# Six tiles of the last projection as three Strassen pairs, between the steps of the sample attention

## The reference, cut to what matters

```
u = rmsnorm(x, norm_w) @ w_in
cq = rmsnorm(u[..., :Q_LORA_RANK], q_norm_w)
gate = u[..., Q_LORA_RANK:]
...
o_lat = mla_attend(q_lat, q_pe, q_pos, c_kv, k_pe, k_pos)
o = jnp.einsum('bthr,rhv->bthv', o_lat, kv_w_uv).reshape(B, T, MLA_GATE_WIDTH)
return x + (o * jax.nn.silu(gate)) @ w_out
```

## Time and profile before

| | |
|---|---|
| median of 3 runs | 1011.04 us (1010.95 to 1015.64) |
| profiled execution, first to last instruction | 1015.5 us |
| TensorE busy | 989.5 us, 97% of the span, 4180 matmul records |
| VectorE, ScalarE, GpSimd busy | 54%, 40%, 43% |
| mean granted TensorE clock | 0.992 |

### The profile page before, as it was taken

How to read it: one execution, slowest core, us unless ns; L and a number is a source line. 1 busy time by engine, 2 the same in 40 slices (tenths; PEclk the granted TensorE clock), 3 DMA queues, 4 the chain that set the end, 5 groups by cost and what they waited for, 6 DMA issues and landing times.

```text
span 1015.5 us, 11585 instructions
## 1 busy us (share of the span) xinstructions
PE 989.5 (97%) x4180; PEld 620.6 (61%) x4180; DVE 548.5 (54%) x1087; ACT 411.2 (40%) x803; POOL 437.0 (43%) x404
## 2 busy tenths in 40 slices
PE   7999999999979999999999999999999999999998
PEld 4666776767645453634546777777666666656655
DVE  5974573755667686877756333253244535443225
ACT  3476877765774635536221000011222423243221
POOL 1576785976524858677321263111530302100110
PEclk9999999999998999999999999999999999999999
DMA  7215234334285999999898122212211111303202
GB/s 274 76 68 182 85 109 158 109 129 140 86 322 218 371 411 369 395 357 380 338 349 306 61 83 83 83 42 107 80 59 35 51 42 45 120 7 127 81 27 103
DMA packets 45576, 164.22 MB, mean 162 GB/s; under 512 B 4996, under 2 KB 8200, under 8 KB 36560
## 3 DMA queue, kind: packets, MB, share of 16 engines
q1 hardware_dynamic: 45520, 163.49, 43.5%
HBM read 106.25 MB, written 57.23 MB: 161 GB/s over the span
## 4 chain that ended last, share of the span: by engine, by line
PE 66%; DVE 2%; POOL 1%; ACT 1%; issue 1%; DMA 0%; SPq 0%; ACTq 0%; POOLq 0%; DVEq 0%
PE work_a L764 6%; PE work_a L1118 6%; PE work_b L1327 5%; PE work_b L764 5%; PE bank L1202 5%; PE work_b L1411 5%; PE work_a L1094 4%; PE bank L1085 3%; PE work_b L1070 3%; PE work_a L1011 3%; PE work_b L1202 3%; PE bank L1372 2%; PE work_a L1397 2%; PE work_a L1357 1%; PE bank L1524 1%; PE work_a L1202 1%
## 5 line engine op out<-in xcount | busy, mean ns | idle before, releaser
L2704 POOL TENSOR_TENSOR arena<-arena 128x640 f32<-128x640 f32 x96 | 138.8, 1463 | 38.6 <-ACT arena L1563 36.1
L2314 DVE SCALAR_TENSOR_TENSOR arena<-arena,bank 128x512 f32<-128x512 f32 x128 | 87.1, 742 | 38.2 <-PE bank L1085 38.2
L2878 POOL COPY arena<-arena 32x640 f32<-32x640 f32 x20 | 16.9, 846 | 123.1 <-ACT arena L1867 116.8
L886 PE MATMUL work_a<-arena 128*128 128x320 f32 x224 | 66.5, 441 | 2.0 <-DVE arena L2079 2.0
L886 PE MATMUL work_a<-arena,ring 128*128 128x320 f32 x224 | 64.9, 432 | 0.0
L1118 PE MATMUL work_a<-arena 128*128 128x512 f32 x128 | 64.1, 613 | 0.0
L886 PE MATMUL work_b<-arena 128*128 128x320 f32 x224 | 62.9, 433 | 0.0
L764 PE MATMUL work_a<-arena,ring 128*128 128x320 f32 x192 | 55.8, 451 | 7.2 <-DMA ring<-in_stream 7.2
L886 PEld LDWEIGHTS work_a<-arena 128*128 128x128 f32 x224 | 43.2, 193 | 20.6 <-issue 3.3
L886 PEld LDWEIGHTS work_b<-arena 128*128 128x128 f32 x224 | 42.9, 191 | 18.0 <-issue 0.4
L886 PEld LDWEIGHTS work_a<-arena,ring 128*128 128x128 f32 x224 | 42.3, 190 | 17.3
(11 more groups left out here) (359 smaller groups left out, 2047.6 us busy)
## 6 DMA issues: line engine op xcount, KB each, us to landing
ring<-in_stream SPq DMA_DIRECT2D x66, 512.0 KB, 3.6
arena<-in_c SPq DMA_DIRECT2D x32, 1024.0 KB, 8.8
out_s_c<-arena SPq DMA_DIRECT2D x32, 1024.0 KB, 7.0
arena<-in_keys SPq DMA_DIRECT2D x8, 664.0 KB, 4.0
z_scratch<-arena SPq DMA_DIRECT2D x16, 320.0 KB, 2.9
v_scratch<-arena SPq DMA_DIRECT2D x20, 256.0 KB, 2.3
k_scratch<-arena SPq DMA_DIRECT2D x4, 1280.0 KB, 5.4
arena<-k_scratch SPq DMA_DIRECT2D x4, 1280.0 KB, 9.1
```

Of the source, the lines that this page charges most:

```text
L886: last = mm(quarter[q], weights[:, k, :], tokens_of[:, k, :], start=fresh and k == 0, stop=k == KH - 1, skip_group_check=True)
L2314: op = v.scalar_tensor_tensor(ct[s % CS][:, g, :], ct[s % CS][:, g, :], decb[:, h, b:b + 1], bank[g][:, :], ALU.mult, ALU.add)
L2704: op = g.tensor_tensor(dst, dst, parts[(adds[0] - adds[1]) % len(parts)], ALU.add)
```

## The change

Tiles 0 and 1 stay as they are (16 k-steps). Tiles 2 to 7 become three pairs m = 1, 2, 3. In a pair the two weight tiles (w0, w1), each split into upper and lower four k-tiles, and the tokens, split at frame 256, form 2 x 2 blocks. Seven products of 4 k-steps at 256 columns take the place of 2 x 8 k-steps at 512 columns. Their names in the order of issue: FIRST, SECOND, OTHER, THIRD, FOURTH, FIFTH, SEVENTH. FIRST and OTHER add up in one half of `work[1]`; otherwise the products take turns between the two halves, so that a product waits until DVE has read the one two before it.

- TensorE: `last_products` is a generator, `fill(n)` takes n k-steps from it. The iterations b = 1 to 6 hand out 5 + 5 k-steps where they handed out 3 + 3; b = 0 hands out 3 + 1 of tiles 0 and 1 and 2 of pair 1; then 8 and 14.
- POOL: `mix_last_weights(m)` makes four sums of weights (128 x 512 each) for a pair: for pair 1 before `keep_own(0)`, for pairs 2 and 3 in the iterations b = 3 and b = 5, behind `keep_own(b + 3)`. `mix_last_tokens` makes four differences of tokens (128 x 1024 each) once: the first needs the upper four tiles of `og`, the others wait until DVE has written all of `og` (`E.free[0]` at 24). It stands between `keep_own(0)` and `keep_own(1)`.
- DVE: `took_last` takes the six results of a pair from PSUM and adds them to `x1` at two or more places; ten instructions for a pair where there were two. ACT: `keep_first(m)` copies FIRST to SBUF before OTHER is added to it. Squares wait for a new signal of a finished tile.

The core of the diff (`last_part`, semaphore sums and buffer places left out):

```diff
-        out_after = {0: (0, 1), 1: (2,), 3: (3,), 4: (4,), 5: (5,)}
+        squares_after = {0: (0, 1), 2: (2,), 3: (3,), 5: (4,), 6: (5,)}
+        took_after = {1: ((1, L_SECOND), (1, L_OTHER)), 2: ((1, L_THIRD), (1, L_FOURTH)), 3: ((1, L_FIFTH), (1, L_SEVENTH)),
+                      4: ((2, L_SECOND), (2, L_OTHER)), 5: ((2, L_THIRD), (2, L_FOURTH), (2, L_FIFTH)), 6: ((2, L_SEVENTH),)}
+        mixed_after = {3: 2, 5: 3}
...
+                for m in range(1, N_STRASSEN + 1):
...
+                    yield from product(m, L_FIRST, w0[:, upper], og[:, upper, left])
+                    if m == 1:
+                        pe.wait_ge(O.free[1], c.all(O.free[1]))
+                        pe.wait_ge(last_mixed, LAST_MIXED + TOKENS_MIXED + 4)
+                    else:
+                        took(m - 1, L_SEVENTH)
+                    pe.wait_ge(last_mixed, LAST_MIXED + W_MIXED[m - 1] + 2)
+                    yield from product(m, L_SECOND, last_w_mix[1], last_x_mix[1])
+                    pe.wait_ge(last_kept, LAST_KEPT + m)
+                    yield from product(m, L_OTHER, w0[:, lower], og[:, lower, left], False)
+                    took(m, L_SECOND)
+                    yield from product(m, L_THIRD, last_w_mix[0], last_x_mix[0])
+                    pe.wait_ge(last_mixed, LAST_MIXED + W_MIXED[m - 1] + 4)
+                    took(m, L_OTHER)
+                    yield from product(m, L_FOURTH, last_w_mix[3], og[:, lower, right])
+                    took(m, L_THIRD)
+                    yield from product(m, L_FIFTH, last_w_mix[2], last_x_mix[2])
+                    took(m, L_FOURTH)
+                    yield from product(m, L_SEVENTH, w1[:, lower], last_x_mix[3])
...
             for b in range(STREAMS - 1):
                 sample_scores(b + 1)
-                out_calls(3)
+                if b:
+                    fill(5)
+                else:
+                    out_calls(3)
                 sample_turn(b)
-                out_calls(3)
+                if b:
+                    fill(5)
+                else:
+                    out_calls(1)
+                    fill(2)
                 sample_outputs(b)
             sample_turn(STREAMS - 1)
-            out_calls(4)
+            fill(8)
             sample_outputs(STREAMS - 1)
-            out_calls(6)
+            fill(14)
...
+            def mix_last_tokens():
...
+                g.tensor_tensor(last_x_mix[0], top_y[:, :, right], top_y[:, :, left], ALU.subtract).then_inc(last_mixed, 1)
+                pool.wait_ge(E.free[0], 6 * PAIRS)
+                pool.wait_ge(last_mixed, LAST_MIXED + TOKENS_MIXED + 1)
+                g.tensor_tensor(last_x_mix[1], low_y[:, :, right], last_x_mix[0], ALU.subtract).then_inc(last_mixed, 1)
+                g.tensor_tensor(last_x_mix[2], low_y[:, :, right], top_y[:, :, right], ALU.subtract).then_inc(last_mixed, 1)
+                pool.wait_ge(last_mixed, LAST_MIXED + TOKENS_MIXED + 2)
+                g.tensor_tensor(last_x_mix[3], low_y[:, :, left], last_x_mix[1], ALU.subtract).then_inc(last_mixed, 1)
...
+                    pool.wait_ge(out_w_in, 16 * (KD - SLOTS))
+                    pool.wait_ge(last_mm, last_done(m - 1, L_FIFTH))
...
-            for b in range(3):
-                keep_own(b)
+            pool.wait_ge(gate_mm, GATE_MM * (PAIRS - 1))
+            pool.wait_ge(rotated, c.all(rotated) + PAIRS)
+            pool.wait_ge(E.free[0], 6 * (PAIRS - 1) + 2)
+            mix_last_weights(1)
+            keep_own(0)
+            mix_last_tokens()
+            keep_own(1)
+            keep_own(2)
             for b in range(STREAMS):
-                for t in out_after.get(b, ()):
+                for t in squares_after.get(b, ()):
                     add_out_square(t)
                 if b + 3 < STREAMS:
                     keep_own(b + 3)
+                if b in mixed_after:
+                    mix_last_weights(mixed_after[b])
```

More of the change, by code:

```diff
@@ L382, in program @@
         uv = take(RT, AH * P)
+        pe_at = top[0]
         pe_raw = take(T)
@@ L1305, in _ @@
             out_order = iter([(t, k) for t in range(2) for k in range(KD - 2)]
[L1306 to L1307 removed]
+                             + [(t, k) for t in range(2) for k in (KD - 2, KD - 1)])
             def out_calls(n):
@@ L1314, in out_calls @@
                     if k == 0:
[L1315 to L1324, removed]
+                        slot = 2 + t
+                        pe.wait_ge(w_in[slot], c.next(w_in[slot], step=16))
+                        pe.wait_ge(E.free[1], c.all(E.free[1]))
+                        pe.wait_ge(gate_out, GATE_OUT * (PAIRS - 1))
                     if t == 0 and k >= KD - 2:
@@ L1331, in out_calls, with last_products, product, took @@
                         c.skip(O.free[w])
+            def last_products():
+                upper, lower, left, right = slice(0, KH), slice(KH, KD), slice(0, QUARTER), slice(QUARTER, SEQ)
+                def product(m, which, weights, tokens_of, fresh=True):
+                    for k in range(KH):
+                        last = mm(last_part(m, which), weights[:, k, :], tokens_of[:, k, :], start=fresh and k == 0,
+                                  stop=k == KH - 1, skip_group_check=True)
+                        if k == KH - 1:
+                            last.then_inc(last_mm, 1)
+                        yield
+                def took(m, which):
+                    pe.wait_ge(last_took, last_read(m, which))
+                for m in range(1, N_STRASSEN + 1):
+                    if m == 1:
+                        w0, w1 = ring[:, 0], ring[:, 1]
+                        for slot in range(2):
+                            pe.wait_ge(w_in[slot], c.next(w_in[slot], step=16))
+                        pe.wait_ge(O.free[0], c.all(O.free[0]))
+                    else:
+                        w0, w1 = out_w[:, 2 * m - 4], out_w[:, 2 * m - 3]
+                        pe.wait_ge(out_w_in, 16 * (KD - SLOTS))
+                        took(m - 1, L_FIFTH)
+                    yield from product(m, L_FIRST, w0[:, upper], og[:, upper, left])
+                    if m == 1:
+                        pe.wait_ge(O.free[1], c.all(O.free[1]))
[15 more added lines that the diff above has]
+                    yield from product(m, L_SEVENTH, w1[:, lower], last_x_mix[3])
@@ L1333, in stage_e, with fill @@
+            last_calls = last_products()
+            def fill(n):
+                for _ in range(n):
+                    next(last_calls)
             def stage_e(p):
@@ L1526, in _ @@
                         pe.wait_ge(out_summed, c.all(out_summed, ahead=KD - 1))
-                        pe.wait_ge(O.free[0], c.all(O.free[0]))
+                        pe.wait_ge(last_took, last_read(N_STRASSEN, L_SEVENTH))
                         op = mm(work[1][:, 0:SEQ], ones_f[:], out_sum, start=True, stop=True)
@@ L2594, in _ @@
                 own_probabilities((b + 1) % 2)
-                for t in out_after.get(b, ()):
-                    add_out(t)
+                if b == 0:
+                    add_out(0)
+                    add_out(1)
+                for m, which in took_after.get(b, ()):
+                    took_last(m, which)
                 keep_sample(b)
-            add_out(KD - 2)
+            for m, which in last_took_early:
+                took_last(m, which)
             keep_sample(STREAMS - 1)
-            add_out(KD - 1)
+            for m, which in last_took_late:
+                took_last(m, which)
             for g in range(2):
@@ L2928, in _, with mix_last_weights @@
                     mix_gate_weights(p)
+            def mix_last_tokens():
+                left, right = slice(0, QUARTER), slice(QUARTER, SEQ)
+                top_y, low_y = og[:, 0:KH], og[:, KH:KD]
+                g.tensor_tensor(last_x_mix[0], top_y[:, :, right], top_y[:, :, left], ALU.subtract).then_inc(last_mixed, 1)
[5 more added lines that the diff above has]
+                g.tensor_tensor(last_x_mix[3], low_y[:, :, left], last_x_mix[1], ALU.subtract).then_inc(last_mixed, 1)
+            def mix_last_weights(m):
+                if m == 1:
+                    w0, w1 = ring[:, 0], ring[:, 1]
+                    for slot in range(2):
+                        pool.wait_ge(w_in[slot], 16 * (NI // 2 + 9))
+                else:
+                    w0, w1 = out_w[:, 2 * m - 4], out_w[:, 2 * m - 3]
+                    pool.wait_ge(out_w_in, 16 * (KD - SLOTS))
+                    pool.wait_ge(last_mm, last_done(m - 1, L_FIFTH))
+                done = LAST_MIXED + W_MIXED[m - 1]
+                g.tensor_tensor(last_w_mix[0], w1[:, 0:KH], w1[:, KH:KD], ALU.add).then_inc(last_mixed, 1)
+                pool.wait_ge(last_mixed, done + 1)
+                g.tensor_tensor(last_w_mix[1], last_w_mix[0], w0[:, 0:KH], ALU.subtract).then_inc(last_mixed, 1)
+                g.tensor_tensor(last_w_mix[2], w0[:, 0:KH], w1[:, 0:KH], ALU.subtract).then_inc(last_mixed, 1)
```

(2 more changed lines are left out.)

72 lines of the change are left out of this document (69 added, 3 removed).

## The result

| | before | changed |
|---|---|---|
| median, 6 runs each | 1011.66 us | 1025.72 us |
| range of the runs | 1010.95 to 1015.64 | 1024.73 to 1029.97 |
| ratio | | 1.0138, 95% interval 1.0118 to 1.0158 |
| profiled execution: time, span | span 1015.5 | 1024.73, span 1023.0 |

The change makes the kernel 14 us slower; +13.2 was forecast. In every run whose time and span are both known, the time is 1.7 to 1.9 us above the span, so the profiled execution before, with its span of 1015.5, took some 1017.3 us and lies about 6 us above the median, not 4.5. The forecast does not move by that: it comes to the median plus 13.2.

The account below looks back on a forecast made before the run. TensorE, busy 989.5 of 1015.5 us, was taken as the bound. Passes saved −4.8, first wait +8.7, second wait +5.7 and clock +3.6 gave +13.2 on the median 1011.04: 1024.2 us, range 1016 to 1030.

Parts of the forecast that it names:

- Passes saved: TensorE's last projection: 96 records of 512 columns removed, 168 of 256 added, saving 4.8 us; no charge for weight loads.
- The Trainium skill's rule on short records: Half-width records: load and matmul together set the distance, so they cost more than their columns; +3 to +32 us, chance 0.02.
- First wait: TensorE's scores of stream 1 wait for `keep_own(1)`, queued on POOL behind the token differences: 8.7 us, ends 8.3 and 9.6.
- Second wait: In b = 4, pair 2's SECOND waits for weight sums queued on POOL behind `keep_own(6)`: 5.7 us, high end 1.0 more.
- The clock: Behind each of the two pauses TensorE runs at half clock: 1.8 us each, 3.6 in all, ends 0 and 6.2.
- My high end of 3.1 us a pause: Upper clock charge, from the program's first 32 records, which took 11.88 us where 32 take 8.78.
- The first rival (the clock holds): Same two waits on TensorE, but no half-clock loss behind them: 1020.6 us; chance 0.12.
- What costs nothing: Pair 1's sums beside pair 3's rope (0 us, at most 0.5), and VectorE's, ScalarE's and POOL's added work: no charge.
- "Nothing" for pair 3's sums: In b = 5, TensorE has 6.5 us of work before needing pair 3's two sums of 2.6 us, so no wait.
- VectorE as a second bound: Rival: VectorE's reads of products come late, 0.5 us in each of seven iterations, +3.5 us, 1027.7; chance 0.12.
- Sum: −4.8 + 8.7 + 5.7 + 3.6 = +13.2 us on the median of 1011.04, giving 1024.2 us.
- the main case's own bounds: All low ends +9.2, 1020.2 us; all high ends +18.2, 1029.2 us; the forecast itself had chance 0.60.

Follow-up runs that it names:

- The version without waits: Changed kernel with own-key copies ahead of token differences, weight sums ahead of squares and key copy, probability scaling on ScalarE: 1007.94 us, ratio 0.9953 to the kernel before.
- the half-width run: Kernel before with each call of the last projection cut into two of 256 columns, no sums: 1012.71 us, ratio 0.9995.
- the keys first: Changed kernel with the copies of own keys of streams 1 and 2 ahead of the token differences on POOL: 1023.93 us, ratio 1.0110 to the kernel before.
- the run with the sums first: Changed kernel with weight sums of pairs 2 and 3 at the start of POOL's iteration, ahead of squares and key copy: 1017.96 us, ratio 1.0054 to before.
- the spare passes: Changed kernel with spare matmuls in both pauses, 9 calls before stream 1's scores and 6 behind stream 5's: 1022.89 us, ratio 1.0084 to the kernel before.
- The run with both moves: Changed kernel with own-key copies ahead of token differences and weight sums at the start of POOL's iteration: 1016.78 us, ratio 1.0034 to the kernel before.

## Why the prediction was right, step by step

- **Passes saved, −4.8.** Held. The version without waits gains 4.6 us in the stretch and 4.4 between the medians. The Trainium skill's rule on short records ("TensorE: Matmul & The Clock Gate", Back-to-back issue gap), as a rival, falls at this width: 0.216 us a record in the half-width run, half of the 0.429 of a record of 512 columns.
- **First wait, 8.7.** 8.2 idle, 8.36 from start to start. I took 2.43 us for a difference of 1024 elements, the middle of two groups early in the program of which one has a mean of 2.52; here each row has 2.34 to 2.39, and 2.31 from start to start. Mechanism shown: with the keys first, the wait is gone.
- **Second wait, 5.7.** 5.78 idle, 5.93 from start to start. Shown by the run with the sums first.
- **The clock, 3.6.** Mis-sized: 1.8 + 2.95 = 4.8. The term for the first pause was exact, the one for the second low by 1.1: behind it the clock stays at 0.50 for some 6 us and not 3.5. Why it stays longer there no run shows. My high end of 3.1 us a pause had no row of the clock behind it either: during the program's first 32 records the trace has a granted clock of 1.00, so no row shows their slowness to be the clock's. Shown to be the clock by the spare passes. The first rival (the clock holds) falls.
- **What costs nothing.** Here I was too generous in one place, and it is the one term of the sum that I put at nothing and that cost something. I looked at POOL beside VectorE only for pair 1's sums, where events keep them apart, as forecast (no wait at L1428 beyond those of before). I wrote "Nothing" for pair 3's sums, and asked only whether they come in time. They do, but they hold VectorE's scaling of stream 7 for 1.7 us (2.23 for 0.49), its next read of a product comes late, and TensorE waits 0.3 us, 0.5 from start to start. In the changed kernel the same hold beside the token differences is hidden in the pause itself; it cost 3.6 us and the clock as soon as the pause was taken away.

The timeline of the changed kernel has VectorE's scaling beside pair 3's sums and the read that came late. POOL's sums there start at 981.49 and 982.71; the second ends at 983.97, some 0.16 us ahead of the scaling (984.13):

```profile
981.90 2.23 DVE L2594 TENSOR_SCALAR arena<-arena 128x16 f32<-128x16 f32 x2
984.05 0.41 DVE L2708 TENSOR_TENSOR arena<-arena,work_b 128x256 f32<-128x256 f32 x1
```

```profile
982.71 1.26 POOL L3093 TENSOR_TENSOR arena<-xc,arena 128x512 f32<-128x512 f32 x1
```

- **VectorE as a second bound** falls as I meant it (by its own work). VectorE's lateness was real, but POOL's doing.
- **Sum.** +13.2 forecast, +14.1 between the medians, +14.8 in the traces. 1024.2 against 1025.72, within the main case's own bounds. By terms, the traces differ from the forecast by −0.3 for the first wait, +0.2 for the second, +1.1 for the clock and +0.5 for VectorE. The two waits missed in opposite directions, but by little, so the sum does not owe its closeness to luck.

## What to carry to other kernels

When one engine is nearly always busy, an edit that saves it passes is worth only what the helpers' queues allow: write down, for each helper instruction that is added, what now stands behind it on its queue and who waits for that. In this kernel it paid to put copies that others wait for ahead of sums that wait for late data, and sums whose data are there ahead of copies that wait for a DMA: the two moves were worth 9 us between the medians and, with one small operation moved to another engine, turned +14 us into −4.4. Price a pause with the half-clock stretch behind it, 1.6 to 3 us here, and before adding sums on GpSimd look at which VectorE instructions read and write SBUF in the same stretch.

## What was not expected of the hardware

- A pair of VectorE scalings, 128 x 16 and 128 x 256, SBUF to SBUF, took 4.13 us beside GpSimd's additions and 0.49 without; its end followed the end of a GpSimd instruction. In the same stretches VectorE's instructions with an operand in PSUM kept their time (maximum 0.43 us for 0.44), and GpSimd's kept theirs (2.34 us in and out of the overlap). It is not always so: in the earlier trace rows a sum of GpSimd that VectorE's L2466 joined 0.8 us after its start took 1.90 us for 1.28, and L2466 itself 1.77 us for 0.82 (the same instruction, L2563, in pair 3 of the changed kernel). The same scalings on ScalarE took 0.71 us beside the same additions.
- The granted clock fell to 0.50 in the second of two idle stretches of 1.8 us with 1.4 us of work between them, and 2.9 us were lost behind them, as much as behind an unbroken pause of 5.8 us. The run with both moves shows the same at the same place, 3.1 us.
